# Decoding the top-16 picks of heads 0 to 3 in the router stage instead of the decode stage

## The reference, cut to what matters

```python
q = (xf @ wq).reshape(t, PEER_HEADS, PEER_QDIM)          # 256 tokens, 8 heads, 2 x 128
s1 = jnp.einsum('thd,kd->thk', q[..., :half], keys1)
s2 = jnp.einsum('thd,kd->thk', q[..., half:], keys2)
v1, i1 = lax.top_k(s1, PEER_TOPK)                         # 16 best of each list
v2, i2 = lax.top_k(s2, PEER_TOPK)
cand_s = (v1[..., :, None] + v2[..., None, :]).reshape(t, PEER_HEADS, -1)
cand_i = (i1[..., :, None] * PEER_KEYS + i2[..., None, :]).reshape(t, PEER_HEADS, -1)
top_s, pos = lax.top_k(cand_s, PEER_TOPK)                 # 16 best of the 256 sums
expert = jnp.take_along_axis(cand_i, pos, axis=-1)
gate = jax.nn.softmax(top_s, axis=-1)
z = x . u[expert];  out = sum over experts of gelu(z) * gate * v[expert]
```

## Time and profile before

| what | us |
|---|---|
| median of 3 runs (2696.03 to 2696.39) | 2696.3 |
| the profiled execution, its own time | 2696.89 |
| its span, first to last instruction | 2695.2 |
| PE busy | 2669.4 |
| DVE busy | 1835.3 |
| ACT busy | 1369.4 |
| POOL busy | 371.4 |

### The profile page before, as it was taken

How to read it: one execution, slowest core, us unless ns; L and a number is a source line. 1 busy time by engine, 2 the same in 40 slices (tenths; PEclk the granted TensorE clock), 3 DMA queues, 4 the chain that set the end, 5 groups by cost and what they waited for, 6 DMA issues and landing times.

```text
span 2695.2 us, 47112 instructions
## 1 busy us (share of the span) xinstructions
PE 2669.4 (99%) x14299; PEld 2298.4 (85%) x14299; DVE 1835.3 (68%) x2985; ACT 1369.4 (51%) x2066; POOL 371.4 (14%) x296
## 2 busy tenths in 40 slices
PE   8999999999999999999999999999999999999998
PEld 6888888898888998888888888888888888888887
DVE  6666665668987677489996777775565555555555
ACT  6454445555665444455455555554444444444444
POOL 0010000001011211011105555551000000000000
PEclk9999999999999999999999999999999999999999
DMA  7566555564554554655567777777976666666564
GB/s 257 189 216 213 181 199 177 177 219 159 172 176 156 167 168 157 195 201 186 195 201 212 202 202 203 201 204 218 305 240 217 217 217 219 212 220 216 200 241 156
DMA packets 204475, 543.26 MB, mean 202 GB/s; under 512 B 37504, under 2 KB 82816, under 8 KB 203392
## 3 DMA queue, kind: packets, MB, share of 16 engines
q1 hardware_dynamic: 148112, 486.74, 54.9%
q10 hardware_dynamic: 35568, 47.33, 5.0%
q0 software_dynamic: 20736, 8.46, 2.7%
HBM read 515.12 MB, written 27.33 MB: 201 GB/s over the span
## 4 chain that ended last, share of the span: by engine, by line
PE 94%; DVE 3%; ACT 1%; issue 1%; DMA 0%; SPq 0%; DVEq 0%; POOL 0%; ACTq 0%; POOLq 0%
PE bank L561 32%; PE bank L568 16%; PE bank L2693 8%; PE bank L2694 8%; PE bank L2695 8%; PE bank L601 4%; PE bank L603 4%; PE bank L602 4%; PE bank L2488 1%; DVE w_lo L504 1%; PE bank L527 1%; PE bank L528 1%; PE bank L529 1%; PE bank L2658 1%; PE bank L2465 0%
## 5 line engine op out<-in xcount | busy, mean ns | idle before, releaser
L504 DVE TENSOR_TENSOR w_lo<-raw,w_hi 128x1024 fp32r<-128x1024 f32 x902 | 1097.9, 1226 | 725.9 <-ACT w_hi L495 719.4
L495 ACT ACTIVATE w_hi<-raw 128x1024 fp32r<-128x1024 f32 x902 | 950.8, 1059 | 946.5 <-PE bank L568 363.1
L561 PE MATMUL bank<-act,w_hi 128*128 128x512 f32 x3840 | 975.2, 396 | 2.6 <-DVE cst L579 1.0
L561 PEld LDWEIGHTS bank<-act,w_hi 128*128 128x128 f32 x3840 | 692.0, 189 | 133.8 <-issue 6.4
L568 PEld LDWEIGHTS bank<-act,w_lo 128*128 128x128 f32 x3840 | 519.7, 190 | 33.1
L568 PE MATMUL bank<-act,w_lo 128*128 128x256 f32 x3840 | 535.6, 282 | 0.0
L2693 PE MATMUL bank<-w_hi,expert_act 128*128 128x512 f32 x1008 | 392.3, 389 | 0.1
L2694 PE MATMUL bank<-w_lo,expert_act 128*128 128x512 f32 x1008 | 392.2, 389 | 0.0
L2695 PE MATMUL bank<-w_hi,expert_act 128*128 128x512 f32 x1008 | 392.1, 389 | 0.0
L742 POOL DMA_INDIRECT g_kept<-slot_t x128 | 239.7, 1872 | 253.8 <-issue 170.4
L2693 PEld LDWEIGHTS bank<-w_hi,expert_act 128*128 128x128 f32 x1008 | 189.3, 188 | 39.6 <-DVE cst L579 0.5
(11 more groups left out here) (344 smaller groups left out, 2498.4 us busy)
## 6 DMA issues: line engine op xcount, KB each, us to landing
raw<-in_stream SPq DMA_DIRECT2D x902, 512.0 KB
z_kept<-cst ACTq DMA_DIRECT2D x112, 128.0 KB, 2.4
cst<-z_kept ACTq DMA_DIRECT2D x112, 128.0 KB, 3.9
g_kept<-zeros POOLq DMA_DIRECT2D x16, 512.0 KB
big<-in_ukv ACTq DMA_DIRECT2D x16, 512.0 KB, 4.6
big<-g_kept SPq DMA_DIRECT2D x16, 512.0 KB, 5.6
big<-in_rows ACTq DMA_DIRECT2D x3, 1024.0 KB, 5.8
big<-in_x SPq DMA_DIRECT2D x2, 1024.0 KB, 10.2
```

The costliest lines, as they stand in the source:

```text
L495: act.activation(w_hi[:, s, :], raw[:, s, :], ACT.Copy).then_inc(hi_ready, 1)
L504: dve.tensor_tensor(w_lo[:, s, :], raw[:, s, :], w_hi[:, s, :].bitcast(F32), ALU.subtract).then_inc(lo_ready, 1)
L561: pe.matmul(bank[:, :], w_hi[:, s, kk * P:(kk + 1) * P], act2[:, k, :, :].rearrange("p a n -> p (a n)"), start=(k == 0), stop=False)
```

## The change

The decode steps become functions of a range of heads: `convert_picks`, `compare_picks`, `index_picks` and `collect_picks`. `early_picks` calls them for heads 0 and 1 during router heads 2 to 4, and for heads 2 and 3 during router heads 5 to 7, in six pieces for each two heads: conversion with the first compare, multiplies, reduction, second compare, multiplies, reduction. Each router head takes one piece after the splits of its pair 2 and one after those of the next head's pair 1. The decode stage converts and decodes heads 4 to 7 alone. Its number of splits between steps falls accordingly, and the rest come after the picks. On ScalarE turn 1 is written out, the exponential comes after it, and the second loop runs turns 2 to 6.

```diff
             early_turn(0, first=True)
-            with act.Fori(1, PH // 2) as i:
-                early_turn(i)
+            early_turn(1)
             act.wait_ge(pick_diff, 1)
             act.activation(CV, CV, ACT.Exp).then_inc(pick_exp, 1)
-            with act.Fori(PH // 2, PH - 1) as i:
+            with act.Fori(2, PH - 1) as i:
                 early_turn(i)
...
+            def convert_picks(lo, hi):
+                cols = slice(lo * wide, hi * wide)
+                step.wait()
+                places = CP[:, lo:hi, :, :].rearrange("p h t k -> p (h t k)")
+                step(dve.tensor_scalar(CAU[:, 0, cols], places, 4, None, ALU.logical_shift_right))
+                step(dve.tensor_scalar(CAU[:, 1, cols], places, 15, None, ALU.bitwise_and))
+                step(dve.tensor_copy(I12F[:, lo:hi, :, :, :].rearrange("p h a t k -> p (h a t k)"),
+                                     I12[:, lo:hi, :, :, :].rearrange("p h a t k -> p (h a t k)")))
+                step.wait()
+                step(dve.tensor_copy(CA[:, :, cols], CAU[:, :, cols]))
...
+            def early_picks(h, first):
+                lo = 2 * ((h - 2) // 3)
+                piece = 2 * ((h - 2) % 3) + (0 if first else 1)
+                a = piece // 3
+                if piece == 0:
+                    convert_picks(lo, lo + 2)
+                if piece % 3 == 0:
+                    compare_picks(a, lo, lo + 2)
+                elif piece % 3 == 1:
+                    step.wait()
+                    for head in range(lo, lo + 2):
+                        index_picks(a, head)
+                else:
+                    collect_picks(a, lo, lo + 2)
+
             for h in range(PH):
                 ahead(split_lo, dve, "wqu", h, 4, 0)
+                if h >= 2:
+                    early_picks(h, True)
                 for a in range(2):
                     ahead(split_lo, dve, "wqu", h, 4, 1 + a)
...
                 ahead(split_lo, dve, "wqu", h, 4, 3)
+                if h >= 2:
+                    early_picks(h, False)
                 for a in range(2):
                     dve.wait_ge(ps_used[a], h + 2)
...
+            half = PH // 2
+            convert_picks(half, PH)
             more(2)
...
+                compare_picks(a, half, PH)
+                more()
+                step.wait()
+                for h in range(half, PH):
+                    index_picks(a, h)
+                    if h % 2:
+                        more()
+                collect_picks(a, half, PH)
+                more()
             dve.wait_ge(pick_exp, 1)
```

More of the change, by code:

```diff
@@ L1993, in top16 @@
                 return dve.max_index(idx[:, 8:16], vals[:, 8:16], work)
+            wide = TT * PK
+            def convert_picks(lo, hi):
[8 more added lines that the diff above has]
+                step(dve.tensor_copy(CA[:, :, cols], CAU[:, :, cols]))
@@ new lines, in compare_picks @@
+            def compare_picks(a, lo, hi):
+                step.wait()
+                step(dve.tensor_tensor(EQ[:, lo * wide * PK:hi * wide * PK].rearrange("p (n j) -> p n j", j=PK),
+                                       CA[:, a, lo * wide:hi * wide].unsqueeze(2)
+                                       .broadcast_to([P, (hi - lo) * wide, PK]),
+                                       iota[:, 0:PK].unsqueeze(1).broadcast_to([P, (hi - lo) * wide, PK]),
+                                       ALU.is_equal))
@@ new lines, in index_picks, with collect_picks @@
+            def index_picks(a, h):
+                eq = EQ[:, h * wide * PK:(h + 1) * wide * PK].rearrange("p (t k j) -> p t k j", t=TT, k=PK)
+                step(dve.tensor_tensor(eq, eq, I12F[:, h, a, :, :].unsqueeze(2).broadcast_to([P, TT, PK, PK]),
+                                       ALU.mult))
+            def collect_picks(a, lo, hi):
+                step.wait()
+                step(dve.tensor_reduce(PICK[:, a, lo:hi, :, :].rearrange("p h t k -> p (h t k)"),
+                                       EQ[:, lo * wide * PK:hi * wide * PK].rearrange("p (n j) -> p n j", j=PK),
+                                       X_AXIS, ALU.add))
@@ L2046, in _ @@
+            convert_picks(half, PH)
             more(2)
-            step.wait()
-            heads = PH // 2
-            width = heads * TT * PK
             for a in range(2):
[L2051 to L2070, removed]
```

## The result

The changed kernel takes 2706.96 us (median of 7 runs, 2705.89 to 2707.76) against 2696.3: a ratio of 1.0039 with the interval 1.0026 to 1.0051. That is 10.7 us slower, where 4.9 us were forecast; the time lies above the range. One run of the kernel before took 3301.91 us beside six of 2696.03 to 2696.79; the comparison leaves it out. The profiled execution took 2707.76 us, its span 2706.1, 10.9 us more than before.

What follows compares the result with a forecast made beforehand. The tensor engine, busy 2669.4 of 2695.2 us, was taken as the bound. Terms 5.40 - 1.87 + 0.1 + 1.3 = +4.9 us on the median of 2696.3 gave 2701.2 us; whole range 2697.5 to 2704.2, own range 2699.5 to 2703.

Steps and rivals of the forecast that it cites:

- What bounds the kernel: Whole kernel: tensor engine busy 2669.4 of 2695.2 us, so other engines' edits can win only its few idle stretches.
- Price of the pieces less the spare time: Router heads 2 to 7, vector engine: added pieces cost 15.3 us; each head has 1.65 us to spare.
- Rival 3: Router stage: pieces cost 18.4 instead of 15.3 us, lag 8.5 us, time 2704.3 us; chance 0.12.
- What hides them: Router heads 2 to 7: spare time hides part of the pieces; the vector engine is 5.40 us behind after head 7.
- plus 5.40: Start of the decode stage: the stalled unit at 1358.26 starts 5.40 us later, at about 1363.66.
- The order of the waits: Router stage: lag free until it passes 4.0 us; tensor engine waits some 0.1 and 0.6 us in heads 6 and 7.
- The clock: Decode stage: after 4.9 us idle the tensor engine restarts at a slower clock, 1.3 us lost, bounds 0 and 2.8.
- Rival 1: Decode stage: the clock stays at full rate over the gap, time 2699.9 us; chance 0.28.
- What is given back: Decode stage: with two quarters instead of four, the four late stalls go, minus 1.87 us.
- The exponential: ScalarE, turns 2 to 6: exponential after two turns, two table loads a turn; 0 to 0.9 us, taken as 0.1.
- rival 4: Loop turns on ScalarE: each table load as long again, five turns cost 3.3 us, time 2704.5 us; chance 0.05.
- The picks: Decode stage: picks published some 18 us earlier, GpSimd's scatters start earlier, which wins nothing as nobody waited for the transposes.

Runs made afterwards that it cites:

- filling the gap: Changed kernel with 20 matmuls of 512 columns into an unused bank behind the fourth unit of the decode stage: 2704.94 us, ratio 1.0031.
- the timed run with fills: Changed kernel, GpSimd's 32 adds replaced by fills of the unused half, scores made from the first half of the query: 2702.85 us, ratio 1.0024.
- with two heads: Half of the change: only the picks of heads 0 and 1 decoded in the router stage, exponential after four turns: 2702.55 us, ratio 1.0018.
- the run with zero scores: Changed kernel, GpSimd's 32 adds replaced by fills with zeros of the same size, sums left out: 3114.96 us, a time that can't be read.

## Why the prediction was wrong

- **What bounds the kernel** was read rightly: nothing but the few idle stretches of the tensor engine could be won, and 1.47 us was.
- **Price of the pieces less the spare time: right.** 15.3 us less 9.9 gives 5.40; without GpSimd's reads the lag was 5.5 us, twice. Rival 3 (dearer pieces) falls by that.
- **What hides them: the step that failed.** The term "plus 5.40" measured 10.0 us. I counted spare time and work of the vector engine, and took each duration as fixed. But the spare time stood behind splits during which GpSimd's adds arrive. Filling it put instructions with two inputs back to back and shifted others under a running add, and an add cost up to 0.55 us of vector time: 4.4 us in ten places. GpSimd stood in the prediction only for its scatters. The hint was in the trace of before: the same add takes 1.29 us in one place and 0.74 in another, with nothing to wait for but the vector engine's split. With the adds' reads gone the rest of the sum held: 2702.85 us in a kernel that leaves those reads out, inside the forecast's own range.
- **The order of the waits** went with it: the lead of the weights gave out in heads 4 to 7 (4.82 us), not in heads 6 and 7 (0.7). The first split of head 7 came 8.8 us late (1340.10 against 1331.51, and 0.25) instead of 4.7. The prediction had named several us of waits there as the sign that it was wrong. Without the adds' reads heads 6 and 7 lose 0.10 and 0.75 us, close to the 0.1 and 0.6 forecast.
- **The clock: right in kind, too small.** 1.3 was taken, 2.5 measured; filling the gap gave back 2.0. The estimate counted seven matmuls at half speed, from the program's start; it was the sixteen of one whole unit, near the prediction's upper bound of 2.8. The price is not one number: with the clock at half for 3.4 us it was 1.4 (the timed run with fills) and 1.6 (each fall with two heads), for 6.8 us it was 2.5. That 1.3 comes close to the 1.4 is luck, as it was read from the program's start. What sets how long it stays low is open. Rival 1 (no fall) is out.
- **What is given back:** three of the four late stalls went, one stayed with 0.40 us: 1.47 instead of 1.87.
- **The exponential:** no wait of the tensor engine for ScalarE in turns 2 to 6. A table load still has its user right behind it (timeline of ScalarE):

```profile
1408.64 1.28 ACT L1195 ACT_TABLE_LOAD   x1
1409.94 0.42 ACT L1195 ACTIVATE cst<-cst 128x256 f32<-128x256 f32 x1
```

  So rival 4 falls; the drain that the Trainium skill ("ScalarE: Activation LUTs", What ACT_TABLE_LOAD costs) adds is not seen here either.
- **The picks** were written 11.3 us earlier (line 2118's copy at 1404.87, line 2087's at 1416.13 before), not 18. The lag was some 4.5 us longer than forecast, and between the add of block 0 and the picks the vector engine waited 4.6 us for ScalarE's high halves, where it had waited 1.3. Nobody waited for the picks, as forecast.

With the measured terms the sum is 10.0 - 1.5 + 2.5 = 11.0 us, against 10.7 between the medians. Shown by experiment are the adds (4.1 us here, 8.0 with two heads, each with what it saves on the clock) and, by the trace rather than by the time, the clock (2.0). The fills are shorter than the adds (0.31 us against 0.74), as well as reading nothing; that the two-input instructions which meet a fill keep their length speaks for the reading, and no run separates the two further. Not settled is which phase of GpSimd's adds against the splits hits how often: ten hits with four heads and fourteen with two are counts, not a rule.

## What to carry to other kernels

Before work is put into the idle time of the vector engine, see what runs on GpSimd in that time: idle time and searches with one input can be the room in which GpSimd's reads pass unnoticed. Where the same instruction shows two durations in one trace, ask what it waits for, and who will wait when the gap behind it is filled. And a long wait of the tensor engine is to be priced with the slower clock that can follow it, not by its length alone.

## What was not expected of the hardware

In these runs a GpSimd add of 256 elements a partition (0.74 us alone) held a two-input instruction of the vector engine by up to 0.55 us, where that instruction stood right behind the split that the add had waited for or began while the add ran. In the kernel before, where a search or idle time followed, it lengthened none. A GpSimd fill (0.31 us) lengthened no two-input instruction, but it held two short conversions by 0.20 and 0.13 us in both runs of the changed kernel with fills. The clock fell to half behind waits of 1.90, 2.12, 4.92 and 5.46 us and stayed full behind waits of 1.63 and 1.68 us; in the run with zero scores it also stayed full behind 2.35 and 2.73 us, so these waits give no threshold.
